# Two late weight chunks of an MoE layer loaded in 32 transfers of eight rows on ScalarE's queue

## The reference

```
h  = x + concat(sliding-window attention, B * conv3(C * hc)) @ w_out
hn = rmsnorm(h)
logits = hn @ w_router + b_router          # 32 experts, top 4 of each token
gu = hn[tokens of e] @ w_gu[e] + b_gu[e]   # 1024 x 2048 for each expert
g  = min(gu[:, :1024], 7);  u = clip(gu[:, 1024:], -7, 7)
a  = (u + 1) * g * sigmoid(1.702 * g)
y  = h + sum over the 4 experts of gate * (a @ w_down[e] + b_down[e])   # 1024 x 1024 for each expert
```

## Time and profile before

| | us |
|---|---|
| median of 3 runs | 1095.98 |
| lowest, highest | 1094.69, 1097.61 |
| the profiled execution | 1097.09 |
| its span, first to last instruction | 1095.3 |
| TensorE busy | 1035.2 |
| VectorE busy | 312.9 |
| ScalarE busy | 97.5 |
| mean granted TensorE clock | 0.985 of full speed |

### The profile page before, as it was taken

How to read it: one execution, slowest core, us unless ns; L and a number is a source line. 1 busy time by engine, 2 the same in 40 slices (tenths; PEclk the granted TensorE clock), 3 DMA queues, 4 the chain that set the end, 5 groups by cost and what they waited for, 6 DMA issues and landing times.

```text
span 1095.3 us, 11585 instructions
## 1 busy us (share of the span) xinstructions
PE 1035.2 (95%) x5069; PEld 492.3 (45%) x5070; DVE 312.9 (29%) x481; ACT 97.5 (9%) x165; POOL 9.3 (1%) x21
## 2 busy tenths in 40 slices
PE   8999999999999999989899999999898989899886
PEld 6767455444444443435343444344343534353333
DVE  3533121322323232322323132313231232323131
ACT  3222130100000000000000010100000000001011
POOL 1100000000000000000000000000000000000000
PEclk9999999999999999999999999999999999999999
DMA  9940769999999999999999999999999999999993
GB/s 350 332 49 1 230 273 383 411 427 428 427 427 426 427 427 427 428 427 425 428 429 425 426 430 427 426 428 427 428 427 426 427 429 425 427 425 420 421 420 114
DMA packets 56818, 420.64 MB, mean 384 GB/s; under 512 B 22900, under 2 KB 23200, under 8 KB 28864
## 3 DMA queue, kind: packets, MB, share of 16 engines
q1 hardware_dynamic: 53744, 418.53, 92.6%
q10 hardware_dynamic: 2672, 0.81, 0.4%
q0 software_dynamic: 352, 0.55, 0.1%
HBM read 418.29 MB, written 1.58 MB: 383 GB/s over the span
## 4 chain that ended last, share of the span: by engine, by line
PE 60%; DMA 38%; DVE 0%; issue 0%; ACT 0%; SPq 0%; DVEq 0%
DMA ring<-in_w_gu_dram 32%; PE ps L773 30%; PE ps L712 6%; DMA ring<-in_w_down_dram 5%; PE ps L635 5%; PE ps L788 4%; PE ps L814 3%; PE ps L653 3%; PE ps L528 2%; PE ps L775 1%; PE ps L799 1%; PE ps L664 1%; PE ps L894 1%; PE ps L538 0%; DMA x<-in_x_prompt_dram 0%; PE ps L604 0%
## 5 line engine op out<-in xcount | busy, mean ns | idle before, releaser
L773 PE MATMUL ps<-ring,xT 128*64 128x512 f32 x1024 | 466.0, 608 | 35.7 <-DMA ring<-in_w_gu_dram 35.1
L775 PE MATMUL ps<-ring,xT 128*64 128x512 f32 x1024 | 466.6, 609 | 0.0
L773 PEld LDWEIGHTS ps<-ring,xT 128*64 128x64 f32 x1024 | 137.9, 140 | 315.8 <-issue 311.0
L788 PE MATMUL ps<-ring,he 128*64 128x512 f32 x480 | 213.7, 595 | 8.1 <-DMA ring<-in_w_down_dram 7.5
L790 PE MATMUL ps<-ring,he 128*64 128x512 f32 x480 | 214.3, 596 | 0.0
L1486 DVE TENSOR_TENSOR x<-ps,x 128x512 f32<-128x512 f32 (+1 forms) x84 | 54.3, 684 | 301.4 <-PE ps L814 273.5
L775 PEld LDWEIGHTS ps<-ring,xT 128*64 128x64 f32 x1024 | 137.9, 140 | 0.0
L788 PEld LDWEIGHTS ps<-ring,he 128*64 128x64 f32 x480 | 62.9, 137 | 139.5 <-issue 139.5
L712 PEld LDWEIGHTS ps<-oh,hn 128*128 128x128 f32 x768 | 95.2, 196 | 9.2 <-issue 6.8
L712 PE MATMUL ps<-oh,hn 128*128 128x128 f32 x768 | 97.4, 282 | 0.0
L1127 ACT COPY gu_sb<-ps 128x1024 f32<-128x1024 f32 x16 | 16.2, 1012 | 593.1 <-PE ps L775 593.1
(11 more groups left out here) (213 smaller groups left out, 594.1 us busy)
## 6 DMA issues: line engine op xcount, KB each, us to landing
ring<-in_w_gu_dram SPq DMA_DIRECT2D x114, 2048.0 KB, 29.3
ring<-in_w_down_dram SPq DMA_DIRECT2D x50, 2048.0 KB, 30.5
ring<-in_w_gu_dram SPq DMA_DIRECT2D x28, 1024.0 KB, 27.7
ring<-in_w_down_dram SPq DMA_DIRECT2D x26, 1024.0 KB, 29.0
w_chc<-in_w_in_dram SPq DMA_DIRECT2D x1, 4096.0 KB, 21.4
w_qkv<-in_w_in_dram SPq DMA_DIRECT2D x4, 768.0 KB, 9.2
w_b<-in_w_in_dram SPq DMA_DIRECT2D x1, 2048.0 KB, 27.6
w_o<-in_w_out_dram SPq DMA_DIRECT2D x2, 1024.0 KB, 27.5
```

The lines of the kernel that those rows point to most:

```text
L773: even = mm(gu_banks(j)[0:CAP, n, :], xT[j % 2][:, k, 0:CAP], ring[:, first % RING, cols], start=(k == 0), stop=(k == KT - 1))
L775: odd = mm(gu_banks(j)[CAP:P, n, :], xT[j % 2][:, k, CAP:P], ring[:, second % RING, cols], start=(k == 0), stop=(k == KT - 1))
L788: even = mm(out[0:CAP, half, :], hid[:, f, 0:CAP], ring[:, first % RING, cols], start=(f == 0), stop=(f == FT - 1))
```

## The change

Chunks 348 and 349 are taken out of SP's `LOADS`. ScalarE issues them instead, in step 14 between the scaling at L1135 and the wait for the end of `gate_up(14, 7)`, after waiting that the chunks before them in their slots have been used. Each is split into 16 DMAs of eight rows (8 partitions of 8 KB), the rows four partitions apart, so 32 DMAs for both; a DMA of eight rows is carried by eight of the 16 DMA engines. For each block of 32 partitions, `r` goes from 0 to 3 and takes partitions r, r + 4, ... r + 28 of it. All 32 raise one new semaphore, `by_rows_in`, and both chunks count as landed when it is at 512. Nothing else is changed; TensorE's order and all other loads stay.

```diff
+        by_rows_in = sem("by_rows_in")
...
         LOADS += [(n, 1) for n in range(ALL - FINE, ALL - 2)]
+        LOADS = [(n, many) for n, many in LOADS if n not in (ALL - FINE, ALL - FINE + 1)]
+
+
+        ROWS = 8
+        BY_ROWS = (ALL - FINE, ALL - FINE + 1)
...
+        for n in BY_ROWS:
+            LANDED[n] = (by_rows_in, 16 * 2 * (P // ROWS))
...
                     scale_y(j - 1, Y)
+                if j == PAIRS - 2:
+
+                    act.wait_ge(chunk_used, max(used_up_to(*ORDER[n - RING]) for n in BY_ROWS))
+                    for n in BY_ROWS:
+                        e, c = ORDER[n]
+                        at = (c - GUC) % 2 * FLAT
+                        for first in range(0, P, 4 * ROWS):
+                            for r in range(4):
+                                rows = slice(first + r, first + 4 * ROWS, 4)
+                                act.dma_start(ring[rows, n % RING, :], dn_dram[e, (c - GUC) // 2][rows, at:at + FLAT]
+                                              ).then_inc(by_rows_in, 16)
                 act.wait_ge(chunk_used, used_up_to(2 * j + 1, GUC - 1))
```

## The result

The changed kernel takes 1107.63 us (median of 4, 1105.77 to 1109.02) beside 1095.34 us of the kernel before on the same chip: ratio 1.0109 [1.0097, 1.0121], about 12 us slower. The forecast was 1101.5 us, its range ended at 1106.8: the sign was right, the size less than half of the true one. A second run gave 1107.71 us, 1.0111 [1.0096, 1.0127].

What follows compares the result with a forecast made beforehand. PE was taken to follow the DMA engines, the last landing setting the end. Only that landing's +5.5 us counted: 1097.09 + 5.5 = 1102.6 us, less 1.1 for the profiled execution, 1101.5 us; 8-in-10 range 1094.8 to 1106.8.

Steps and rivals of the forecast that it cites:

- What bounds the kernel: Whole kernel: PE follows the DMA engines; the end is its last load wait, ending at 1069.56 us, plus fixed work.
- Bytes by engine: Two chunks moved from 16 engines to eight: by engine time alone, eight engines 4.9 us later, eight 4.9 us earlier.
- Where the rows are written: Rows to partitions 64 to 127 share a limited port: loaded eight +9.9 us, relieved engines gain nothing; 285 GB/s for 15 us.
- Which engine is then last: DMA tail: a middle engine of the eight moves from 1074 to 1075.5 to 1084 to 1085.4; last landings 5.5 us later.
- Rival 1: DMA tail: the last engine is among the eight, its end moves from 1079 to 1088.9: +9.9, 1105.9 us; chance 0.18.
- The way there: From issue near 963.5 to 988 us: rows done near 988 without a wait; PE stands about 11 us, not added to 5.5.
- Issue costs: ScalarE's 32 DMA issues, 0.38 to 0.57 us each, 12 to 18 us in all, hidden in its idle time: no cost.
- Rival 2: Partitions 64 to 127 have room, turns do not double, a middle engine is among the eight: 1096.5 us; chance 0.23.
- Rival 3: DMA tail: the change evens out the engines without an upper-half wait, 3.5 to 4.5 us faster: 1092 us; chance 0.12.

Runs made afterwards that it cites:

- the two lower kernels: Changed kernel with only rows of partitions 0 to 63 of both chunks loaded by rows, upper halves left out: once, 1093.52 us; loaded twice, 1099.26 us.
- the one with single loads: Changed kernel with the 22 chunks ahead of the two loaded one by one, 8 KB packets instead of 16 KB: 1105.45 us, ratio 1.0094.
- the upper and the lower kernel: Changed kernel loading only one half's rows of both chunks: partitions 64 to 127, 1102.29 us; partitions 0 to 63, 1093.52 us.
- the lower rows twice: Changed kernel without the upper halves, lower halves loaded again once the first have landed: 1099.26 us, ratio 1.003.
- the lower rows only: Changed kernel with only rows of partitions 0 to 63 of both chunks loaded, 1 MB left out: 1093.52 us, ratio 0.9979.
- the stages alone: Kernel before plus six load stages after its outputs, no compute engine working: 430 GB/s with lower rows, 334 with upper, 271 with adjacent, 215 to 64 partitions alone.

## Why the prediction was wrong

*What bounds the kernel*: right. Last wait at 1079.90, +10.3, span +10.3; PE's work unchanged.

*Bytes by engine* (+4.9 and -4.9): right for the loaded eight, by themselves 5.6 us between the two lower kernels. The relief of the others is seen only beside the loss, in the change's first part (3.3 = 8.2 - 4.9).

*Where the rows are written*: right in kind, and mis-sized. The step priced the meeting in the upper half at 16 x 0.31 = 5.0 us for the loaded eight and at 4.9 us, their whole relief, for the others. Measured it is 8.2 us for each: the eight come to +13.1 instead of +9.9, the others to +3.3 instead of 0. The forecast of the rate had the same 5.0 in it, 285 GB/s for 15 us being 15 x 142/427. The rate was nearly right (305 and 301); the 15 us were not, they were 29. They stood on rows getting half of their engine. The queues' lines (packets, MB, share of 16 engines) of the changed kernel from 977 to 992 and from 998 to 1012, then of the one with single loads from 971 to 981:

```profile
q1 hardware_dynamic: 362, 3.97, 87.0%
q10 hardware_dynamic: 147, 0.60, 13.1%
...
q1 hardware_dynamic: 501, 3.65, 86.9%
q10 hardware_dynamic: 137, 0.54, 13.6%
```

```profile
q1 hardware_dynamic: 339, 2.47, 85.5%
q10 hardware_dynamic: 133, 0.53, 16.8%
```

q10 is ScalarE's. Its rows moved at 40 GB/s in the first slow stretch, where most of SP's bytes are in 16 KB packets, at 39 in the second, where they are in 8 KB ones, and at 53 in the kernel with single loads; half of eight engines would be over 70 even at 300 GB/s in all. So the step gave the rows too large a share of their engines. That a packet of 16 KB takes twice the turn of a row is one part of it; why the rows of the second stretch are as slow beside 8 KB is not settled.

*Which engine is then last*: the second step that failed, and it cost as much. The forecast let a middle engine of the eight decide, one that ended at 1074 to 1075.5, 3.5 to 5 us ahead of the last, and so turned +9.9 into +5.5. Rival 1 put the last engine itself among the eight, at 0.18, and had 1105.9 us. By the table above neither holds: the slowest of the eight was some 1 to 3 us ahead of the last. The forecast and the time are 11.9 - 5.5 = 6.4 us apart; 3.2 of it is the meeting (8.2 in place of 5.0), and the other 3.2 is this head start, 1.2 us in the sum of the change where the forecast had 4.4. The time is near rival 1's, but not for rival 1's reason: its +9.9 had the smaller meeting in it.

In the profiled executions the last wait moved by only 10.3 us, where the medians moved by 12: on its last engine the changed kernel's ran 1.0 us ahead at chunk 324 already, and in that of the kernel before the last engine loses a further 1.6 us after chunk 375. What makes single engines lag by such amounts was not settled. One candidate, not tested, is in the traces: the instruction queue's packets of 16 KB keep one engine for 1.0 to 1.2 us each, and one of them starts at 1061.5 us in the kernel before.

*The way there*: the issue began at 961.7 (forecast 963.5). The forecast had the rows done near 988 without a wait for them; they landed at 1012.24 and PE waited for them. It wanted 8 to 12 us of waits before the down product of 988.42; there were 2.2 + 6.55 = 8.8 us, and that product started at 997.52, 9.1 us late. Behind this wait the clock was granted at 0.50, the 1.2 GHz level, as after the wait of the earlier trace rows:

```profile
997.52 1.09 PE L796 MATMUL ps<-ring,he 128*64 128x512 f32 x1 [6.55 <-DMA ring<-in_w_down_dram]
...
997.00:1003.00 6.00, 5.48 (x14) 1.91 (x16) 0.00 (x0) 0.00 (x0) 0.00 (x0) 0.50 1.03 305
```

That later waits take up this stall and the last landing sets the end was right.

*Issue costs*: hidden, as forecast, though an issue took 0.66 us and not 0.38 to 0.57.

Rival 2 (the upper half has room) is refuted by 300 GB/s and by 8.8 us between the upper and the lower kernel. Rival 3 (faster, by evening out the tail) falls with the first engines being later. Its idea does not come out without upper rows either: with the lower rows twice, which moves as many bytes as the kernel before, the time is 3.3 us longer, so the slowest of the eight have too little in hand for 4.9 us more. No run here beats the kernel before by doing its whole work.

## What to carry to other kernels

When sixteen engines are all busy on a stream, work given to some of them must be priced on two sides: their own time, and where their rows go. Here rows of partitions 0 to 63, four apart, cost only engine time; rows of 64 to 127, or adjacent ones, slowed every load in flight for as long as they were under way. How long that is must be measured or bounded from a run, and not taken from an even share of the engine: it was 29 us in place of 15. And where the end hangs on the slowest engine, the unevenness in the tail says that it matters who is loaded, but not who that is. A harmless load on the suspects tells it: their old share alone (the lower rows only), and then twice that, each against the kernel before.

## What the runs showed of the hardware

Rows of partitions 64 to 127 that eight engines carry beside a full stream bring it from 427 GB/s to between 301 and 327 in the kernel (298 and 334 in the stages alone), while all engines read as busy; rows of 0 to 63, four apart, leave it at 420 to 430. The loss for all sixteen engines is near 0.5 us per upper row of one of the eight (8.2 us for 16 rows each), and 6.1 us for the same rows where SP's loads ahead of them are single. A DMA of 64 rows into the upper half, in the place of eight such, costs about the same (7.7 us). With adjacent rows in all 32 DMAs the loss is 18.6 us, more than twice that of rows four apart. A DMA of eight rows took ScalarE 0.66 us to issue. Of the Trainium skill's page "DMA: Bandwidth & Descriptors" (section on queues, rings and completion order), which has an engine finish a whole packet of 9 to 17 descriptors of one queue before it turns to the other, these runs show less: with eight descriptors of 16 KB against one of 8 KB the rows would have had a seventeenth of their engines' bytes, and they had 0.60 of some 2.3 MB (half of the 4.57 that all sixteen moved) from 977 to 992 us, a quarter.
